# Five norms carried out on the products instead of on their input, and half of two attention out projections placed beside the last heads

## What is computed

```python
# block 1, layer 0 (mixer out_e), then layer 1 (mixer diff attention, out_o)
hn = rms_norm(h, ln_mix);  h = h + mixer(hn) @ w_out
hn = rms_norm(h, ln_mlp);  h = h + square(relu(hn @ w_mlp1)) @ w_mlp2
gate = sigmoid(rms_norm(h, ln_ple) @ w_ple_gate)
h = h + (p @ w_ple_proj) * gate
# block 2, layer 0 (conv + hgrn2, out_ab), layer 1 (stick breaking attention, out_c)
x = x + gate1 * mixer(rms_norm(x, norm_mix) * (1 + scale1) + shift1)
x = x + gate2 * square(relu(hn2 @ mlp_w1)) @ mlp_w2      # hn2: normed, scaled, shifted
# rms_norm(x, g) = x * rsqrt(mean(x * x) + eps) * g, over the channels of a token
```

## Time and profile before

| | |
|---|---|
| three runs | 2927.68, 2929.67, 2932.3 us; median 2929.67 |
| the profiled execution | 2928.48 us, its span 2926.7 us |
| busy | TensorE 2724.2 us (93%), VectorE 1456.0 (50%), GpSimd 1499.1 (51%), ScalarE 800.1 (27%) |
| granted clock of TensorE, mean | 0.971 |
| memory | 268.22 MB read, 92 GB/s over the span |

### The profile page before, as it was taken

How to read it: one execution, slowest core, us unless ns; L and a number is a source line. 1 busy time by engine, 2 the same in 40 slices (tenths; PEclk the granted TensorE clock), 3 DMA queues, 4 the chain that set the end, 5 groups by cost and what they waited for, 6 DMA issues and landing times.

```text
span 2926.7 us, 33461 instructions
## 1 busy us (share of the span) xinstructions
PE 2724.2 (93%) x12309; PEld 2147.9 (73%) x12309; DVE 1456.0 (50%) x1748; ACT 800.1 (27%) x1380; POOL 1499.1 (51%) x815
## 2 busy tenths in 40 slices
PE   5788989999999988999998999899999998899999
PEld 3567768888766666888876877688887665678887
DVE  4355647765344443766534467633333766443222
ACT  4343330111224452111012135311112666221111
POOL 3322337767544334767663544466665333356664
PEclk8999999999999999999999999999999999999999
DMA  4211136653222112655431221233332111123332
GB/s 112 58 37 37 42 103 194 197 168 122 80 65 60 56 44 87 208 175 171 149 101 58 87 65 51 64 99 96 94 100 79 51 50 51 58 85 95 97 97 72
DMA packets 423037, 271.81 MB, mean 93 GB/s; under 512 B 9738, under 2 KB 408980, under 8 KB 422932
## 3 DMA queue, kind: packets, MB, share of 16 engines
q1 hardware_dynamic: 404928, 216.03, 25.3%
q10 hardware_dynamic: 18004, 54.32, 5.5%
HBM read 268.22 MB, written 2.10 MB: 92 GB/s over the span
## 4 chain that ended last, share of the span: by engine, by line
PE 87%; DVE 5%; ACT 5%; issue 2%; ACTq 0%; PEld 0%; DVEq 0%; PEldq 0%
PE ps L407 13%; PE ps L408 12%; PE ps L409 12%; PE pair L407 8%; PE pair L409 8%; PE pair L408 8%; PE ps L1572 2%; PE ps L1574 2%; PE ps L1573 2%; PE ps L736 2%; PE ps L738 2%; PE ps L737 2%; PE pair L1197 1%; DVE arena L518 1%; PE pair L1708 1%
## 5 line engine op out<-in xcount | busy, mean ns | idle before, releaser
L370 POOL TENSOR_TENSOR w_lo<-w_raw,w_hi 128x1024 fp32r<-128x1024 f32 x404 | 985.0, 2438 | 1390.9 <-PE ps L409 721.3
L364 POOL TENSOR_SCALAR w_hi<-w_raw 128x1024 fp32r<-128x1024 f32 x404 | 527.2, 1305 | 10.4 <-DMA w_raw<-in_w_in_e_dram 10.4
L407 PE MATMUL ps<-x_hi,w_hi 128*128 128x512 f32 x1088 | 455.5, 419 | 57.5 <-DVE x_lo L691 37.8
L408 PE MATMUL ps<-x_lo,w_hi 128*128 128x512 f32 x1088 | 436.8, 401 | 0.0
L409 PE MATMUL ps<-x_hi,w_lo 128*128 128x512 f32 x1088 | 435.5, 400 | 0.0
L817 ACT ACTIVATE tt<-sq 128x512 f32<-128x512 f32 x128 | 81.0, 633 | 1070.9 <-DVE sq L850 1070.9
L407 PEld LDWEIGHTS ps<-x_hi,w_hi 128*128 128x128 f32 x1088 | 211.0, 194 | 122.4 <-issue 72.2
L844 DVE TENSOR_TENSOR m_lo<-tt,m_hi 128x512 fp32r<-128x512 f32 x128 | 256.3, 2008 | 0.0
L409 PEld LDWEIGHTS ps<-x_hi,w_lo 128*128 128x128 f32 x1088 | 212.1, 195 | 46.9
L408 PEld LDWEIGHTS ps<-x_lo,w_hi 128*128 128x128 f32 x1088 | 212.9, 196 | 45.4 <-issue 5.8
L518 DVE SCALAR_TENSOR_TENSOR arena<-arena,small 128x1024 f32<-128x1024 f32 x84 | 206.9, 2464 | 0.4
(11 more groups left out here) (368 smaller groups left out, 4334.4 us busy)
## 6 DMA issues: line engine op xcount, KB each, us to landing
w_raw<-in_w_mlp_dram SPq DMA_DIRECT2D x128, 512.0 KB, 4.1
w_raw<-in_mlp_w_dram SPq DMA_DIRECT2D x128, 512.0 KB, 3.9
arena<-in_ada_w_dram ACTq DMA_DIRECT2D x96, 512.0 KB, 4.1
w_raw<-in_w_in_ab_dram SPq DMA_DIRECT2D x28, 512.0 KB, 3.7
w_raw<-in_w_in_e_dram SPq DMA_DIRECT2D x24, 512.0 KB, 3.8
w_raw<-in_w_qkv_o_dram SPq DMA_DIRECT2D x24, 512.0 KB, 3.7
w_raw<-in_w_qkv_dram SPq DMA_DIRECT2D x24, 512.0 KB, 3.7
w_raw<-in_w_ple_gate_dram SPq DMA_DIRECT2D x16, 512.0 KB, 3.9
```

The costliest lines, as they stand in the source:

```text
L364: nc.gpsimd.tensor_scalar(w_hi[:, j, :, :], w_raw[:, j, :, :], 1.0, 1.0, ALU.mult, ALU.mult).then_inc(w_cut_hi, 1)
L370: nc.gpsimd.tensor_tensor(w_lo[:, j, :, :], w_raw[:, j, :, :], w_hi[:, j, :, :].bitcast(F32), ALU.subtract).then_inc(w_ready, 1)
L407: nc.tensor.matmul(bank[:, :], w_hi[:, j, k, :], hi[:, k, :], start=(k == 0), stop=False)
L408: nc.tensor.matmul(bank[:, :], w_hi[:, j, k, :], lo[:, k, :], start=False, stop=False)
```

## The change

Norms 1 to 5 lose their stage. RAW_INTO says into which pair of tiles each goes (norms 1 and 2 into x, 3 to 5 into m), and the second mlp and the first attention swap x and m for that. As each h tile is final, ScalarE, after its square, writes the high half of h times gain, and VectorE the low half. The sums of the norm stand inside the first pair of the next stage, ahead of k = 5; rstd goes into a tile of its own (rs) and is applied where VectorE takes products out of PSUM: in the mlp's relu, before the ple's sigmoid (which now works in place), and in attention for q, k and v, which VectorE now takes instead of ScalarE. The first quarter of mlp0 and mlp1 is unrolled on TensorE. out_o and out_c have half 0 beside items (6,2) to (7,3), in bank ps[0]; v of head 7 moves to item (6,1).

```diff
-        def dense_pair(pe, first, second, hi, lo, rhs_ready, wide=False):
+        def dense_pair(pe, first, second, hi, lo, rhs_ready, wide=False, within=None):
             for k in range(ND + 3):
+                if k == 5 and within is not None:
+                    within()
...
+        X, M = (x_hi, x_lo), (m_hi, m_lo)
+        RAW_INTO = {1: X, 2: X, 3: M, 4: M, 5: M}
+        FULL = [0, 6, 7, 8, 9]
...
             nc.scalar.activation(squares(k), h[:, k, :], ACT.Square).then_inc(*norm_act(f"sq{k}"))
+            if i in RAW_INTO:
+                nc.scalar.activation(RAW_INTO[i][0][:, k, :], h[:, k, :], ACT.Identity, scale=norm_gain(i, k)[0]
+                                     ).then_inc(raw_hi, 1)
+
+        def raw_low(v, i, k):
+            if i in RAW_INTO:
+                hi, lo = RAW_INTO[i]
+                v.wait_ge(raw_hi, ND * (i - 1) + k + 1)
+                nc.vector.scalar_tensor_tensor(out=lo[:, k, :], in0=h[:, k, :], scalar=norm_gain(i, k)[0],
+                                               in1=hi[:, k, :].bitcast(F32), op0=ALU.mult, op1=ALU.subtract
+                                               ).then_inc(raw_lo, 1)
...
             if k >= 2:
                 norm_add(v, i, k - 1)
+            if k >= 1:
+                raw_low(v, i, k - 1)
+            if k == ND - 1:
+                raw_low(v, i, k)
...
+        def norm_root(act, i):
+            act.wait_ge(*norm_pe.at(i, "sum"))
+            nc.scalar.activation(rb[:, 1, :], norm_bank(i)[:, :], ACT.Ln, scale=1.0 / D, bias=eps_col
+                                 ).then_inc(*norm_act("ln"))
+            act.wait_ge(*norm_act.at(i, "ln"))
+            nc.scalar.activation(rs[:, :], rb[:, 1, :], ACT.Exp, scale=-0.5).then_inc(*norm_act("rstd"))
...
+        def half_bank(name, half, n):
+            return ps[0] if in_bank_0(name, half) else ps[n % 2]
...
+                if k == 0 and in_bank_0(name, half):
+                    pe.wait_ge(*(half_added(name, half, n - 1) if n else freed(q - 1, 3)))
...
+            if i < 3:
+                pe.wait_ge(out_added, out_count(OUTS[i], 1, 6))
+            for u, q, quarter in mlp_quarters(pe, i, i < 2):
+                dense_pair(pe, (q, 0), (q, 1), *inner, normed(norm_before), wide=True,
+                           within=first_sum if isinstance(quarter, int) else None)
...
+                    if norm_before in RAW_INTO:
+                        nc.vector.scalar_tensor_tensor(out=relu[:, n % 2, :], in0=ps[n % 4][:, :], scalar=0.0, in1=rs[:, :],
+                                                       op0=ALU.max, op1=ALU.mult).then_inc(bank_free[n % 4], 1)
...
+            def logits(n):
+                v.wait_ge(*done(q + n // 4, n % 4))
+                nc.vector.tensor_tensor(ple_gate[:, n % 2, :], ps[n % 2][:, :], rs[:, :], ALU.mult
+                                        ).then_inc(bank_free[n % 4], 1)
+            v.wait_ge(*norm_act.at(norm_before, "rstd"))
+            logits(0)
             for n in range(8):
-                v.wait_ge(*freed(q + n // 4, n % 4))
+                if n < 7:
+                    logits(n + 1)
+                v.wait_ge(ple_open, 8 * i + n + 1)
                 v.wait_ge(*ple_pe.at(i, f"proj{n}"))
...
+        OUT_BESIDE = {(6, 2): ([(0, range(0, 2))], [(0, range(2, 4))]), (6, 3): ([(1, range(0, 2))], [(1, range(2, 4))]),
+                      (7, 0): ([(2, range(4))], [(3, range(4))]), (7, 1): ([(4, range(0, 2))], [(4, range(2, 4))]),
+                      (7, 2): ([(5, range(0, 2))], [(5, range(2, 4))]), (7, 3): ([(6, range(4))], [(7, range(4))])}
+        def out_ends(u, i, place):
+            return [n for n, ks in OUT_BESIDE.get((u, i), ([], []))[place] if ks[-1] == 3]
...
+            def rooted(self, v, x, w):
+                if w >= 8:
+                    return
+                q, j = self.chunk(x, w)
+                v.wait_ge(*done(q, j))
+                bank = ps[1] if (x, w) == ("k", 0) else ps[0]
+                buf = {"q": self.q[w % 2], "k": self.k[w % 2], "v": self.v if w < 7 else sq[:, 0, :]}[x]
+                nc.vector.tensor_tensor(buf, bank[:, :], rs[:, :], ALU.mult).then_inc(bank_free[j % 4], 1)
...
                                                op1=ALU.add).then_inc(*at_share("diff"))
+                for n_out in out_ends(u, i, 0):
+                    add_half(v, "out_o", 0, n_out, 1.0)
+                if g == 0:
+                    f.rooted(v, "k", 1)
+                if i == 2:
+                    f.rooted(v, "q", u + 2)
                 maxima(g + 2)
+                if i == 0 and u < 7:
+                    f.rooted(v, "v", u)
+                if (u, i) == (6, 1):
+                    f.rooted(v, "v", 7)
+                if i == 3:
+                    f.rooted(v, "k", u + 2)
                 if i == 0 and u < 7:
                     f.q_normal(v, u + 1, q_gain_o)
                     eye(u + 1)
...
                 if i == 2 and u:
                     rest(u - 1)
+                for n_out in out_ends(u, i, 1):
+                    add_half(v, "out_o", 0, n_out, 1.0)
```

More of the change, by code:

```diff
@@ L41 @@
 LEVELS = 7
+LAST_QUARTER = "last"
 class Steps:
@@ L193, in program @@
         gates_b = sb("gates_b", [P, 8])
+        rs = sb("rs", [P, T])
         x_load, small_load, iota_done = sem("x_load"), sem("small_load"), sem("iota_done")
@@ L341, in with_ada @@
         def with_ada(i, quarter):
-            return i < 2 and not isinstance(quarter, int)
+            return i < 2 and quarter is not LAST_QUARTER
         def ada_pieces_at(n):
@@ L717, in out_count, with in_bank_0 @@
             return 4 * (2 * OUTS.index(name) + half) + n // 2 + 1
+        def in_bank_0(name, half):
+            return half == 0 and name in ("out_o", "out_c")
+        def half_bank(name, half, n):
+            return ps[0] if in_bank_0(name, half) else ps[n % 2]
         def half_part(pe, name, half, n, places, mixed=None):
             q, j = quads[name] + half, n // 2
+            bank = half_bank(name, half, n)
+            hi, lo = X if name == "out_o" else M
             for k in places:
@@ L749, in add_half @@
             v.wait_ge(*half_done(name, half, n))
-            nc.vector.scalar_tensor_tensor(out=h[:, n, :], in0=ps[n % 2][:, :], scalar=gate, in1=h[:, n, :],
-                                           op0=ALU.mult, op1=ALU.add).then_inc(bank_free[n // 2] if n % 2 else out_added, 1)
+            nc.vector.scalar_tensor_tensor(out=h[:, n, :], in0=half_bank(name, half, n)[:, :], scalar=gate,
+                                           in1=h[:, n, :], op0=ALU.mult, op1=ALU.add
+                                           ).then_inc(bank_free[n // 2] if n % 2 else out_added, 1)
         def project_tensor(pe, name, mixed):
-            if name not in ("out_e", "out_ab"):
-                for n in range(8):
-                    half_part(pe, name, 0, n, range(4), mixed)
             for k in range(4):
@@ L770, in project_vector @@
         def project_vector(v, name, layer2, next_norm):
-            if name not in ("out_e", "out_ab"):
-                for n in range(8):
-                    add_half(v, name, 0, n, gate_col(layer2, 0, n))
             for n in range(8):
@@ L1567, in part @@
                 q, j = self.chunk(x, w)
+                hi, lo = self.tiles
                 if ks[0] == 0:
@@ L1578, in parts @@
             def parts(self, pe, u, i, half):
+                if (u, i) in OUT_BESIDE:
+                    for n, ks in OUT_BESIDE[u, i][half]:
+                        half_part(pe, self.out, 0, n, ks)
+                    return
+                if (u, i) == (6, 1):
+                    return self.part(pe, "v", 7, range(4 * half, 4 * half + 4))
                 x, w, ks = ((("v", u, range(0, 4)), ("v", u, range(4, 8))),
@@ L1625, in squared @@
                 buf, root, c = (self.q[w % 2], self.q_rooted, 0) if x == "q" else (self.k[w % 2], self.k_rooted, 1)
-                self.taken(act, x, w, buf)
+                if not self.raw:
+                    self.taken(act, x, w, buf)
                 act.wait_ge(*freed(*self.chunk(x, w)))
@@ L2044, in stick_vector @@
                 last.then_inc(*st_item("sum"))
+                for n_out in out_ends(*divmod(g - 1, NT), 1):
+                    add_half(v, "out_c", 0, n_out, gate_col(1, 0, n_out))
                 if i == 1 and u:
@@ L2055, in stick_vector @@
                                         ).then_inc(*st_item("lw"))
+                for n_out in out_ends(u, i, 0):
+                    add_half(v, "out_c", 0, n_out, gate_col(1, 0, n_out))
+            add_half(v, "out_c", 0, 7, gate_col(1, 0, 7))
             rest(7)
@@ L2506, in program @@
         if has("mlp1"):
-            plan += [("loose", norm(4)), ("loose", mlp(1, 4, 5))]
+            plan += [("loose", mlp(1, 4, 5))]
         if has("ple1"):
-            plan += [("loose", norm(5)), ("loose", ple(1, 5, 6))]
+            plan += [("loose", ple(1, 5, 6))]
         if has("conv"):
```

177 lines of the change are left out of this document (103 added, 74 removed).

## The result

The changed kernel takes 2900.8 us (median of 4 runs, 2897.1 to 2902.2) against 2929.6 for the kernel before, run beside it; the ratio is 0.9896, 95% interval 0.9883 to 0.9909. Forecast were 2893.3, with a range of 2870 to 2912. The profiled execution is the fastest of the four: 2897.1, span 2895.3. It lies 31.4 under the profiled one of before, the medians 28.8.

What follows compares the result with a forecast made beforehand. TensorE, 87% of the chain, was taken as the bound. Norms 37.6, heads -16.2, tails 4 and 11 sum to 36.4 off the profiled 2928.5: 2892.1, 2893.3 as a median; range 2870 to 2912.

Steps and rivals of the forecast that it cites:

- Norms: Raw tiles in norms 1 to 5 save 16.0, 12.2 and 10.7, less 1.3 at norm 6: 37.6 us gained.
- The wait of 0.9: Norm 3, ple0 into attention: TensorE reaches the sum about 0.9 us before VectorE's last square is done.
- The low halves: VectorE's raw low halves in the norms: covered, put at nothing; 3.4 us per norm if the cover were gone.
- Heads: Attention, heads 0 to 5: VectorE's order lengthens heads 1 to 5 by 3.0 each, head 0 by 1.2; cost 16.2 us.
- eye "0.2": In an attention head, VectorE's eye step behind q_normal takes 0.2 us.
- Rival (a): VectorE's order does not bite in attention, takings slip into idle time: 2870 us; chance 0.18.
- q_normal's size: In attention's heads q_normal is held up under GpSimd's cut; if not, the cost is 1.3 a head, not 3.0.
- Attention's tail: Half 0 of out_o fills TensorE's gaps in the last heads; half 1 starts at 1129.5, not 1133.7: gain 4.
- Stick's tail: Half 0 of out_c runs beside stick's last items; half 1 starts at 2524.6 instead of 2535.3: gain 11.
- (b): Low halves and moved waits eat half of the norms' gain, or the tails give nothing: 2911 us; chance 0.13.
- (c): First products do not run on raw tiles in time, norms and their clock give nothing: 2931 us; chance 0.03.
- (d): Attention's new gaps let TensorE's clock fall in every head, 9 us a head: 2956 us; chance 0.06.

Runs made afterwards that it cites:

- the doubled run: Every raw low half of norms 1 to 5 computed twice, the second waiting for the first, on the changed kernel: 2912.7 us.
- the run with v later: On the changed kernel, attention's VectorE takes v in the head's second item, behind the shares (head 7's in (6,2)): 2872.9 us.
- with q_normal out of the way: On the changed kernel, q_normal and eye stand ahead of the taking of v in attention's first item: 2895.6 us.
- the half behind: On the changed kernel, half 0 back behind its stage: out_o behind attention 2910.4 us; in another run, out_c behind stick 2912.7 us.
- the kernel with both fillers: The run with v later plus stick's next-item steps ahead of tile waits and attention's second add behind the next shares: 2870.1 us.

## Why the prediction was right

The direction, the range and the mechanism held; the measured time is 7.5 us over the forecast, in the upper part of the forecast's own range of 2878 to 2907. By the traces 5.0 of the 7.5 are in the terms: 3.0 in the heads, 1.6 for a slow stretch in mlp0 that no term had, 1.5 in stick's tail and 0.6 in attention's, less 1.4 that the norms gave more and 0.3 of the rest.

**Norms.** Forecast 37.6, found 39.0 at the stages' own marks: 8.0, 6.5, 11.2, 14.4 for two, -1.1. The sum of the pair's products, two fp32 sums and a slow first matmul was right to 0.1 in norm 1. Of its 8.0, the part that the slow clock made is not fixed: with 6 slow matmuls in place of 14 norm 1 is worth 6.8. The wait of 0.9 that was set against norm 3 did not come: the sum issues at 842.39 and waits for nothing. The low halves cost nothing; the doubled run shows how near that was.

**Heads.** Forecast 16.2, found 19.2. The step that was mis-sized is eye "0.2": it took 0.99 under GpSimd's second cut. The prediction had named that cut, at 0.7 us, and not counted it. That is 0.8 of a head, less 0.3 to 0.4 that the other pieces came out shorter; head 0 lost 2.1 for the 1.2 forecast. Rival (a), that the order does not bite, fell; the run with v later shows that it is the order, by removing it: the heads go from 32.4 to 29.1, 0.2 over the kernel before. That q_normal's size mattered was only half right: with q_normal out of the way a two-column operation and the next one pay nearly the same.
The Trainium skill, SBUF — State Buffer, "Who interferes with whom", names more than the two-input case that the prediction used: a tensor_scalar can enter the two-port modes and then contends too, and a tensor_reduce, or an instruction with at most one SBUF input outside those modes, does not. Here eye and the two-column lam, both tensor_scalar with a single input tile, were held up (0.99, 1.74), the maxima under a cut took 0.42, and the taking, with one input in PSUM and one in SBUF, 0.69: the traces agree. Applied to the second cut, which ends at 1038.44, that half of the rule would have given eye its 0.99.

**Attention's tail.** Forecast 4, found 3.4, by a working that had the gap in (6,1) and turned_o under the cut. It is a small difference of two large terms, 12.1 won and 8.7 given back, where the prediction had 16 and 12; that the difference came out so near is in part luck. So is its starting point: half 1 of out_o stands at 1134.76 in the trace of before, not at the 1133.7 of the working. With the half beside the heads the order accounts for the second term whole (9.3 in the run with v later), with the half behind for 3.9 of 8.9; the rest of that case is open but for its clock.

**Stick's tail.** Forecast 11, found 9.5, and 11.9 by the medians of the kernel with the half behind. The step that came out longer is the last. In the clock of the profile before (norm 8's sums laid on each other) VectorE starts the adds of tiles 2 to 6 at 2501.0, 2504.9, 2511.5, 2516.4 and 2520.3, forecast 2500.7, 2504.4, 2511, 2516 and 2519.5, but tile 7's at 2524.2, forecast 2522.3: tile 7 uses the same bank and begins behind tile 6's add, which the working had left out.

**From trace to median.** The terms sum to 31.4 in the profiled executions, the medians differ by 28.8, because the profiled one is the fastest of its four: that is the rest of the 7.5. Rivals (b), (c) and (d) fell: no wait on raw tiles, products at a granted clock of 1.00 from the first, and 1.00 in heads 1 to 5 as well.

## What to carry to other kernels

When one event releases two engines that share something, look at what stands next in each one's written order: the first instruction there that contends pays, be it 512 columns wide or two. Put work that is ready ahead of the wait, and behind it what does not contend. A step moved onto an engine with idle time is hidden only if nothing that others wait for stands behind its wait, and a gain elsewhere in the change (here 39 us of norms) covers such a loss until one edit isolates it. Price a part by undoing it in the final kernel too: the difference of two traces gave out_o's half 3.4 us, where it was worth 10 to 14.

## What was not expected of the hardware

**Short slow stretches of TensorE behind a wait of half a microsecond.** A kernel's executions differ by several microseconds. In the profiled run of the kernel with both fillers (2877.8, the slowest of its five) norm 1 to norm 2 took 371.0 us, where the kernel with v later took 367.8, and norm 4 to norm 5 371.0, where that one took 366.2: together 8.0, about the 7.7 between this execution and its median. TensorE's timeline there, with the one-column fp32 products of ada_w, and two windows (columns as above):

```profile
588.77 2.25 PE L511 MATMUL pair<-ones,arena 128*128 128x1 f32 x16 [0.53 <-DVE small L531]
590.87 0.77 PE L409 MATMUL pair<-m_hi,w_hi 128*128 128x512 f32 x1
591.45 0.63 PE L410 MATMUL pair<-m_lo,w_hi 128*128 128x512 f32 x1
```

```profile
590.00:598.00 8.00, 8.00 (x26) 6.47 (x26) 0.00 (x0) 0.00 (x0) 1.77 (x2) 0.57 0.23 66
1400.00:1407.00 7.00, 7.00 (x20) 5.50 (x20) 0.00 (x0) 0.00 (x0) 0.77 (x1) 0.57 0.26 75
```

TensorE is busy throughout both windows, yet the granted clock is 0.57: near the 1.2 GHz level for 14 matmuls, then back. The stretches follow those narrow fp32 products; which of them have one, and how long, changes from one trace to the next (the changed kernel has one at 498 that the trace of before does not have, its 1.6 us in the table). The narrow products alone are not enough. Each trace has twelve groups of 16: six follow the product before them with no idle time, as this one of the changed kernel,

```profile
466.13 1.84 PE L511 MATMUL pair<-ones,arena 128*128 128x1 f32 x16
```

and six stand behind a wait of 0.44 to 0.54 us for VectorE, as at 588.77. In the 13 traces of this study none of the 78 without the wait is followed by a slow stretch, and 42 of the 78 with it are. No run takes the wait away, so this is a count and not a test of the cause.

**A two-column operation that takes 1.74 us.** Its 128x2 elements cost 0.23 when GpSimd is idle. Under the cut (971.15 to 973.53) it starts at 971.80 and ends at 973.54, with the cut, as a 128x512 one does; the reciprocal of the same two columns just before it is not held up.
